# Attention scores of two transformer layers: full fp32 matmuls replaced by split queries and keys in three fp32r products

## What is computed

```python
def attend(qg, keys, vals):      # 8 query heads of 128, 2 key/value heads (4 query heads share one)
    s = jnp.einsum('bqkgd,bskd->bkgqs', qg, keys, preferred_element_type=jnp.float32) * (HEAD_DIM ** -0.5)
    p = jax.nn.softmax(s, axis=-1).astype(vals.dtype)
    return jnp.einsum('bkgqs,bskd->bqkgd', p, vals)
def latent_attention(q, k, v, kc, vc):
    keys = jnp.concatenate([kc, k], axis=1)      # 256 context keys and 512 latent keys
    vals = jnp.concatenate([vc, v], axis=1)
def context_attention(qc, kc, vc):               # context queries see context keys only; not in the last layer
    ...
```

## Time and profile before

| | us |
|---|---|
| runs: median (lowest, highest) | 3069.18 (3058.85, 3069.38) |
| profiled execution, its own time | 3058.82 |
| its span | 3057.0 |
| TensorE busy in the span | 2832.9 (93%) |
| VectorE, ScalarE, GpSimd busy | 1546.1, 999.5, 476.3 |
| attention of layer 0, layer 1 in the span | from 1831 to 1972, from 2731 to 2853 |

### The profile page before, as it was taken

The page is one execution under the profiler, slowest core; times in us unless marked ns, Lnnn a source line. Parts: engine busy times, 40 slices in busy tenths (PEclk is TensorE's granted clock), DMA queues, the critical chain, the costliest instruction groups (busy, mean ns, idle before and its releaser), DMA issues. The chain is left out here.

```text
span 3057.0 us, 35970 instructions
## 1 busy us (share of the span) xinstructions
PE 2832.9 (93%) x13890; PEld 2216.1 (72%) x13890; DVE 1546.1 (51%) x2122; ACT 999.5 (33%) x1689; POOL 476.3 (16%) x585
## 2 busy tenths in 40 slices
PE   7899999988548999999999999899989999989897
PEld 5666666667225877888888887688878877867785
DVE  6677878866554454115542426522243275546334
ACT  4444444444343334112221216511143222226321
POOL 2544444425011113000000002200010000002000
PEclk9999999999659999999999999999999999999999
DMA  5578777763123224223323323222223354451421
GB/s 194 182 300 316 281 302 295 303 226 139 37 88 111 95 99 153 85 103 129 117 96 138 128 95 134 107 80 95 75 91 105 125 176 147 150 181 59 158 96 55
DMA packets 111685, 447.17 MB, mean 146 GB/s; under 512 B 11440, under 2 KB 19760, under 8 KB 76208
## 3 DMA queue, kind: packets, MB, share of 16 engines
q1 hardware_dynamic: 111536, 445.16, 39.9%
HBM read 375.25 MB, written 69.86 MB: 146 GB/s over the span
## 5 line engine op out<-in xcount | busy, mean ns | idle before, releaser
L2734 PE MATMUL ps<-h_hi,w_hi 128*128 128x512 f32 x1600 | 576.9, 361 | 0.0
L2735 PE MATMUL ps<-h_lo,w_hi 128*128 128x512 f32 x1600 | 565.1, 353 | 0.0
L2736 PE MATMUL ps<-h_hi,w_lo 128*128 128x512 f32 x1600 | 561.4, 351 | 0.0
L386 PE MATMUL ps<-h_hi,w_hi 128*128 128x512 f32 (+1 forms) x1152 | 412.9, 358 | 35.7 <-DVE w_lo L345 35.7
L387 PE MATMUL ps<-h_lo,w_hi 128*128 128x512 f32 (+1 forms) x1152 | 412.0, 358 | 0.0
L388 PE MATMUL ps<-h_hi,w_lo 128*128 128x512 f32 (+1 forms) x1152 | 409.8, 356 | 0.0
L2734 PEld LDWEIGHTS ps<-h_hi,w_hi 128*128 128x128 f32 x1600 | 301.9, 189 | 49.8 <-issue 6.2
L2735 PEld LDWEIGHTS ps<-h_lo,w_hi 128*128 128x128 f32 x1600 | 301.7, 189 | 46.6 <-issue 6.2
L2736 PEld LDWEIGHTS ps<-h_hi,w_lo 128*128 128x128 f32 x1600 | 300.7, 188 | 43.5
L2512 DVE TENSOR_TENSOR w_lo<-raw,w_hi 128x2048 fp32r<-128x2048 f32 x64 | 146.4, 2287 | 311.4 <-ACT w_hi L2415 311.4
L386 PEld LDWEIGHTS ps<-h_hi,w_hi 128*128 128x128 f32 x1152 | 219.9, 191 | 70.7 <-DVE w_lo L345 38.7
(11 more groups left out here) (391 smaller groups left out, 4726.6 us busy)
## 6 DMA issues: line engine op xcount, KB each, us to landing
raw<-w_in SPq DMA_DIRECT2D x112, 1024.0 KB, 5.2
raw<-ada_w SPq DMA_DIRECT2D x96, 1024.0 KB, 8.3
raw<-w_out SPq DMA_DIRECT2D x48, 1024.0 KB, 5.0
proj<-xw SPq DMA_DIRECT2D x60, 384.0 KB, 2.6
xw<-proj SPq DMA_DIRECT2D x70, 256.0 KB, 3.4
xw<-proj SPq DMA_DIRECT2D x46, 384.0 KB, 3.3
xw<-resid SPq DMA_DIRECT2D x8, 1536.0 KB, 12.5
proj<-wide SPq DMA_DIRECT2D x32, 256.0 KB, 10.9
```

The source lines that it names most:

```text
L386: pe.matmul(a_[q], wh, h_hi[:, h0 + k, lo:hi], start=k == 0, stop=False)
L2734: pe.matmul(a_[q], wh, h_hi[:, k, a:b], start=k == 0, stop=False)
L2735: pe.matmul(a_[q], wh, h_lo[:, k, a:b], start=False, stop=False)
L2736: ins = pe.matmul(a_[q], wl, h_hi[:, k, a:b], start=False, stop=k == KC - 1)
```

## The change

The scores' two operands are split as the weights are. A query tile's high part is copied by ScalarE (`query_high`) and its low part subtracted by GpSimd (`query_low`); a key tile's by ScalarE and, for the first key, VectorE, for the second GpSimd. The parts lie in `w_hi` and `w_lo`, which the attention block does not use otherwise. Three fp32r products replace each fp32 one. In the list of ScalarE the copy of head i + 1's query stands in the first step of head i, behind `exp(g + 2)`; in the list of GpSimd its subtraction stands in the second step. TensorE's wait for loads becomes a wait for the low parts, and SyncE's wait before a query load becomes one for the low part of the query two heads before.

```diff
+            hi_flat, lo_flat = (w[:].rearrange("p a n -> p (a n)") for w in (w_hi, w_lo))
+            q_hi, q_lo, k_hi, k_lo = ([w[:, (z + q) * W:(z + q + 1) * W] for q in range(2)]
+                                      for z in (0, 2) for w in (hi_flat, lo_flat))
...
                         if i:
-                            if i > 1:
-                                sp.wait_ge(s_ready.h, s_ready.at(nu * (i - 1)))
+                            sp.wait_ge(q_low.h, q_low.at(i - 1))
                             sp.dma_start(q_sb[i % 2][:, 0:width], proj2[i][:, 0:width]).then_inc(loaded[i % 2].h, 16)
...
                         if g % nu == 0:
-                            pe.wait_ge(loaded[i % 2].h, loaded[i % 2].at(16 * (i // 2 + 1)))
-                            pe.wait_ge(loaded[2 + kv].h, loaded[2 + kv].at(16))
+                            pe.wait_ge(q_low.h, q_low.at(i + 1))
+                            pe.wait_ge(k_low.h, k_low.at(kv + 1))
                         pe.wait_ge(exp_done.h, exp_done.at(g - 1))
                         for a in range(0, nk, T):
                             b = min(nk, a + T)
-                            ins = pe.matmul(s_ps[g % 2][:, a:b], q_sb[i % 2][:, q0:q0 + P], k_sb[kv][:, k0 + a:k0 + b],
-                                            start=True, stop=True)
+                            s = s_ps[g % 2][:, a:b]
+                            pe.matmul(s, q_hi[i % 2][:, q0:q0 + P], k_hi[kv][:, k0 + a:k0 + b], start=True, stop=False)
+                            pe.matmul(s, q_hi[i % 2][:, q0:q0 + P], k_lo[kv][:, k0 + a:k0 + b], start=False, stop=False)
+                            ins = pe.matmul(s, q_lo[i % 2][:, q0:q0 + P], k_hi[kv][:, k0 + a:k0 + b], start=False, stop=True)
...
+                    def query_low(i):
+                        pool.wait_ge(q_high.h, q_high.at(i + 1))
+                        pool.tensor_tensor(q_lo[i % 2][:, 0:width], q_sb[i % 2][:, 0:width], q_hi[i % 2][:, 0:width].bitcast(F32),
+                                           ALU.subtract).then_inc(q_low.h, 1)
+
+                    def key_low(kv):
+                        pool.wait_ge(k_high.h, k_high.at(kv + 1))
+                        pool.tensor_tensor(k_lo[kv], k_sb[kv], k_hi[kv].bitcast(F32), ALU.subtract).then_inc(k_low.h, 1)
+                    query_low(0)
                     for g in range(total):
+                        if g % nu == 1 and g // nu + 1 < HEADS2:
+                            query_low(g // nu + 1)
+                        if g == nu + 1:
+                            key_low(1)
                         if g % 2 and g > 4:
                             low((g - 5) // 2)
...
+                    def query_high(i):
+                        act.wait_ge(loaded[i % 2].h, loaded[i % 2].at(16 * (i // 2 + 1)))
+
+                        act.wait_ge(s_ready.h, s_ready.at(nu * (i - 1)))
+                        act.activation(q_hi[i % 2][:, 0:width], q_sb[i % 2][:, 0:width], ACT.Copy).then_inc(q_high.h, 1)
+
+                    def key_high(kv):
+                        act.wait_ge(loaded[2 + kv].h, loaded[2 + kv].at(16))
+                        act.activation(k_hi[kv], k_sb[kv], ACT.Copy).then_inc(k_high.h, 1)
+                    query_high(0)
+                    key_high(0)
                     exp(0)
                     exp(1)
                     v_out(0)
...
                         if g + 2 < total:
                             exp(g + 2)
+                        if g % nu == 0 and g // nu + 1 < HEADS2:
+                            query_high(g // nu + 1)
+                        if g == nu:
+                            key_high(1)
...
+                    dve.wait_ge(k_high.h, k_high.at(1))
+                    dve.tensor_tensor(k_lo[0], k_sb[0], k_hi[0].bitcast(F32), ALU.subtract).then_inc(k_low.h, 1)
                     peak(0)
                     peak(1)
```

More of the change, by code:

```diff
@@ L201, in program @@
         low_ready, low_ready_v = count("low_ready"), count("low_ready_v")
+        q_high, q_low, k_high, k_low = (count(n) for n in ("q_high", "q_low", "k_high", "k_low"))
         odd_copied, shifted = count("odd_copied"), count("shifted")
@@ L1756, in layer_attention @@
             for s, v in ((loaded[0], 64), (loaded[1], 64), (loaded[2], 16), (loaded[3], 16), (loaded[4], 32), (loaded[5], 64),
-                         (loaded[6], 64), (mixd_in, 16 * HEADS2), (mixd_hi, HEADS2), (mixd_lo, HEADS2), (s_ready, total),
+                         (loaded[6], 64), (mixd_in, 16 * HEADS2), (mixd_hi, HEADS2), (mixd_lo, HEADS2), (s_ready, total), (q_high, HEADS2), (q_low, HEADS2), (k_high, 2), (k_low, 2),
                          (neg_max, total), (exp_done, total), (p_ready, total), (t_ready, total), (t_out, total),
```

## The result

The changed kernel takes 3077.97 us (median of 9 runs, 3073.19 to 3083.74), the kernel before 3067.29 us (median of 9 runs, 3058.85 to 3071.38): ratio 1.0041, 95% interval [1.0027, 1.0055]. That is 10.7 us slower, a clear difference, and less than the 0.5% taken for a limit.

A forecast was written before the change was run, and what follows sets the result against it. TensorE bounds the kernel, with a VectorE-ScalarE ring 0.9 us behind in layer 0. Layer 0 +5.0 and layer 1 +4.8 give +10 us, 3079 against the median 3069.18; range 3066 to 3096, no difference, leaning to slower.

The forecast's parts named there:

- The two mechanisms: Head 1's query load exposed in layer 0 (stage +5.0 us) and query handovers in layer 1 (stage +4.8 us).
- Step 1: Scores in both layers: cheaper products save TensorE 16.5 us, 1.1 a head in layer 0 and 0.96 in layer 1.
- cap in layer 0: VectorE-ScalarE work keeps layer 0's head period from falling much below 15.1 us; 15.57 taken, 0.42 saved a head.
- Step 2: Split before the first scores: TensorE starts 2.7 us later in layer 0, 2.2 in layer 1, covered by a later wait.
- Step 3: Layer 0: ScalarE's copy blocks on head 1's query load, queued behind weights; head 1 +7.3 us, stage +5.0.
- seven heads at -0.42: Layer 0: the heads' cheaper scores give back 2.9 us of head 1's delay.
- Step 4: Layer 1 handovers: copy and subtraction follow each query's landing; head 1 +2.1, six handovers +3.6, last head -0.9, together +4.8 us.
- the middle, 13.6: Layer 1's head period through the query-load loop, taken between 14.2 and 12.9 us; +0.6 for each of six handovers.
- The port: Rival: GpSimd subtractions and VectorE normalisations block each other, 3.4 us in layer 0, about 2.5 in layer 1; +16, chance 0.27.
- The clock: Rival: TensorE's clock falls at every layer 1 handover, 1.7 us each, +11 more, so +21; chance 0.13.
- The load in time: Rival: the second query's load lands by 1842, layer 0 loses nothing at its start; total about -5 us, chance 0.11.
- the second ring: VectorE-ScalarE cycle from maximum to normalisation, 2.93 us a latent unit; about 15.1 us a head in layer 0, 11.7 in layer 1.

The follow-up runs named there:

- e1: Kernel before with three fp32r products in place of each fp32 score product, nothing split, no wait added; ratio 0.9977, layers 138.8 and 119.2 us.
- e8: e7 with the queries' low parts subtracted by VectorE instead of GpSimd; ratio to the kernel before 1.0111, layers 148.3 and 149.6 us.
- e3: Changed kernel with loads of head 1's query and the second key issued ahead of the weight loads; ratio to the kernel before 1.0002.
- e10: e7 with each query's copy and subtraction one step earlier from head 2 on; ratio to the kernel before 0.9955, layers 145.1 and 114.4 us.
- e5: Changed kernel with each query load from head 2 on issued ahead of the gate's wait on SyncE; ratio to the kernel before 1.0033.
- e7: Changed kernel with both load changes, those of e3 and e5; ratio to the kernel before 0.9992, layers 145.6 and 121.9 us.
- e9: e7 with GpSimd's query low part subtracted for one column only; ratio to the kernel before 0.9954, layers 143.6 and 113.8 us.
- e11: e10 with head 0's scores left in fp32 on the unsplit tiles; 3049.22 us, ratio to the kernel before 0.9943, layers 141.7 and 112.1 us.
- e2: Changed kernel with scores in fp32 from unsplit tiles again, split and its waits kept, SyncE's old wait added; ratio to the kernel before 1.0056.

## Why the prediction was right, point by point

The forecast was +10 us, 3079; measured were +10.7 and 3077.97. The two mechanisms are the ones that were named, and the parts compare so, with layer 0 like for like.

- **Step 1, the saving.** 1.1 and 0.96 us a head on TensorE, and a cap in layer 0 at 15.57. e1: 15.52 and 12.1. Right; the whole 16.5 us never was to be had. The 15.57 was the middle of two bounds, 15.1 and 16.0, and that it fits to 0.05 is luck.
- **Step 2, the first split.** 2.7 us forecast, 3.5 measured in layer 0 (TensorE idle for 6.56 instead of 3.04), of which 0.8 because the first key's low part waited for GpSimd (e8); 2.2 forecast and 2.8 measured in layer 1 (5.20 instead of 2.43). Hidden, as said, and 3.3 us in the open as soon as the load is early (e3).
- **Step 3, head 1 of layer 0.** +7.3 forecast, 27.2 - 19.6 = +7.6 measured; ScalarE's wait of "some 4 us" is 3.93, and the clock fell behind it as forecast (granted 0.66 from 1856 to 1861). But the stage's +5.0 was too low: like for like it is +6.9. The step that failed is "the second key's split costs about 0.6 once" with "seven heads at -0.42". Head 1 took 16.87 and head 2 16.19 us where the steady ones have 15.64: 1.8 us and not 0.6, and a steady head gains 0.36. From head 1 to head 7 only 0.3 us came back. The 1.8 are not the key's split alone: e10, which splits the key in the same steps but the queries one step earlier, has 15.85 and 15.77 us where its steady heads have 15.76. It is key and query split in the same steps that costs.
- **Step 4, layer 1.** +2.1 forecast for head 1, 21.27 - 19.39 = +1.9 measured. The six handovers were sized at +3.6 and cost +5.2; the last head gave back 0.8 of 0.9. The size that was off is "the middle, 13.6": steady heads took 14.0. The loop through the load is real (e5), but it is one of two bounds. The other, that copy and subtraction stand too late in their queues even with the load there, I had not seen. It alone holds the steady heads at 12.96 (e7), and e10 removes it.
- **Rivals.** The port: the blocking is there, as the rows above show, but costs a steady head of layer 0 nothing (15.64 us with and without it, e9). At most the 1.1 us of heads 1 and 2 are its, a third of the 3.4 that I put on layer 0. The clock: not in the kernel after, where six waits of 0.6 to 1.9 us left it at 2.4 GHz (the first matmul behind them takes 0.50 us; behind the wait of 6.56 us 0.77). But the rival was nearer than this looks: of the nine waits of 1.8 to 2.0 us before a head's first scores in layer 1, over all profiles, four were followed by a fall (e3, e5, e7, e11), and the same wait of 1.96 us had one in e7 and none in e10. The load in time: e3 made it so, and the program came to 1.0002, above my -5, because the first split then shows in layer 0 and the handovers of layer 1 stay.
- **The chances.** The measured 0.35% stands on the side that was called likelier. That it stands at the forecast to 1 us is luck: layer 0 and 1 were 1.9 and 1.5 us too low, 9.8 together against 13.2 (11.5 as profiled), and the program's interval, 8 to 17 us, holds all of these.

## What to carry to other kernels

When work is put in front of a transfer's first use, look where in that engine's list the new wait stands, and what is queued behind it: a load that nobody waited for cost 4.3 of the 7.6 us by which head 1 came later, because its reader moved four units up. A saving on the busiest engine is only worth what the second ring lets through, so measure the operation alone (e1) and the new waits alone (e2) before judging either; here a change that lost 11 us was 26 us by the stages from what the same idea gives with the loads and the splits in other places and the first head left alone. And compare stage lengths in the profile where the program's runs spread as wide as the effect, but look at the granted clock of both first: one fall more or less is 1.7 us.

## What the runs showed of the hardware that was not expected

The clock can differ between two profiles of the same sequence. The last twelve passes of layer 0 took 4.51 us in the kernel before and 2.83 in the kernel after, with 0.95 us of idle time ahead of them in both; five of the thirteen profiles had them at the half clock, e5 among them and e7, with the same last heads, not. The wait of 1.96 us before head 1 of layer 1 was followed by a granted clock of 0.51 in e7 and 1.00 in e10. Either is worth 1.7 us in a stage length, and why the one profile has it and the other has not stays open. And a normalisation of VectorE that starts inside a GpSimd subtraction is not slowed but held to its end (one of 0.35 us took 1.71), while a maximum that reads PSUM is not held (0.95).
